# Band attention in a streaming encoder step: more projection steps behind a pair's first scores, a sigmoid gate made from the exponential, the attention outputs stored first

## The chip, the cores and the metric

The kernel runs on one core of one Trainium2 chip. The metric is the device time of the program in microseconds (us), as the median of the runs shown. The program is one launch that evaluates two encoder layers; the change touches one stage of it, the band attention of layer 0, which fills about 855 us of the span.

## The reference, cut to what matters

Layer 0 projects the normalised input to a mixer A (gated DeltaNet) and a mixer B (band attention). Only mixer B is touched:

```python
q_b = rms_norm(q_b.reshape(n_b, L, 16, 64), b_q_g)
k_b = rms_norm(k_b.reshape(n_b, L, 16, 64), b_k_g)
# a frame reads its own chunk of 64 and the 8 chunks before it
o_b = softmax(q k^T / 8 + bias(relative distance)) v
o_b = o_b.reshape(n_b, L, B_W) * jax.nn.silu(z_b)
# outputs also: the last 512 rows of k_b and v_b (and the 32 new rows of the sample group)
```

There are 1024 prompt frames and 32 sample frames (1056 columns in all), everything in float32. silu(z) is z / (1 + exp(-z)).

## The kernel before, in words

`band(...)`  works on 8 pairs of heads, `pair(n, p, more)`, with two sets of buffers (`p` is 0 or 1). While TensorE does the attention of pair n it also computes the projections of pair n+1. The two kinds of work are woven together by hand:

- The attention of a pair has 17 units (`UNITS`), one for each chunk of 64 queries and one for the sample group. For a unit u TensorE does `scores(u)` (q k^T into PSUM tile `SC`), later `turn(u)` (transposes of the softmax weights `E` into `PT`, and into `PX` if there are five blocks), and one unit later `values(u)` (into `PX`).
- VectorE does `negate(u)` (bias added, running minimum, into `NS`; L1862), `weigh(u)` (a reciprocal of the row sums, L1878, and the scaling of `E`, L1880) and `gate(u)` (the product of the attention output with the gated `zs`, written to `OF`; L1900). ScalarE does `soften(u)` (the exponential, L1749) and `copy_turned(u)` (PSUM to SBUF, L1759).
- The projections are a list of 39 jobs, `STREAM`: 28 products (names P1, P5, P6, P3, P7, P2, P4 in this order, for query/key (x=0) and gate/value (x=1), each in two halves of the columns), and the transposes and sums `ck`, `n`, `ko`, `vt`. A product has four steps, another job one step: 123 steps a pair. Each step issues two matmul records in the profile. The jobs use two PSUM banks in turn, so a job may begin only when the job two before it has been evicted: `evicted(pe, n, m - 2)`. P1, P5, P6 and P4 are evicted by ScalarE (L1681), P3, P7 and P2 are added by VectorE (L1805).
- TensorE takes steps of this list by `fill(k)`: `FIRST` steps behind each of the first two scores (3 and 3), then `FILL` in each unit (2 behind the transposes, 2 behind the next scores, 2 behind the values). What is left over is done at the end of the pair. ScalarE and VectorE follow the same counts through `steps_at(u)`, so that each evicts a job where TensorE has passed it.
- ScalarE's `gate(n, p)` (L1731) applies Silu to `zs[p]` (128x1056) when the last projections of pair n have been evicted, ahead of that pair's first `soften`. Silu is in another table set than Exp, so a table is loaded before and after it (L1731, L1732).
- TensorE's code is written out for all pairs. ScalarE runs pairs 1 to 6 as a loop of three turns of two pairs, VectorE and SyncE (SP) pairs 1 to 4 as a loop of two turns; SP's queue issues all DMA of the stage.
- SP's order for pair n, in `follow` and `pair`: the next weights of x=0 after P4 of (0,1), bias and cached keys, the next weights of x=1 after P4 of (1,1), the stores of keys (two DMAs, L1459 and L1460) and values (two, L1462 and L1463), then the store of `OF` (L1471), then the cached values. VectorE's `gate(0)` of the next pair waits for the store of `OF` (`st_o`).

Of the kernel before, what the change touches and what calls it, by code (L numbers as in the profile page):

```python
# [15 lines left out]
NTOK = NP + NS  # L16
# [1241 lines left out]
def band(nc, ident, ones, eps, hT, W, w_ld, w_in, q_g, k_g, rel_bias, cache_k, cache_v, bias_rows,  # L1258
# [6 lines left out]
    with ExitStack() as ctx:  # L1265
# [51 lines left out]
        t_made, w_made, padded = sem("t_made"), sem("w_made"), sem("padded")  # L1317
        z_ok, bias_ok = sem("z_ok"), sem("bias_ok")
        s_done, ns_ok, e_ok, ri_ok, p_ok = sem("s_done"), sem("ns_ok"), sem("e_ok"), sem("ri_ok"), sem("p_ok")
# [24 lines left out]
        NORMS = 5  # L1344
        T_FIRST, T_OPS = {"P5": 2, "P6": 3, "P7": 1, "P4": 4}, 9

# [34 lines left out]

        FIRST, FILL, FILL_LAST = (3, 3), (2, 2, 2), (2, 2, 1)

        def steps_at(u, fill=FILL):

            return sum(FIRST) + sum(fill) * u

# [26 lines left out]
        with nc.Block() as block:  # L1414
            @block.sync
            def _(sp):
# [14 lines left out]
                def follow(n, p, more):  # L1431
                    sp.wait_ge(proj_done, n * J + place["P4", (0, 1)] + 1)
                    for j in (0, 1):
                        if more:
                            load_w(n + 1, j)
                        elif more is False:
                            early_w(sp, W, early_ld, w_out, j, BAND_SLOT[j])
                    if more:
                        sp.wait_ge(bias_ok, n + 1)
                        load_bias(n + 1)  # L1440
                        load_keys(n + 1)
                    sp.wait_ge(proj_done, n * J + place["P4", (1, 1)] + 1)
                    for j in (2, 3):
                        if more:
                            load_w(n + 1, j)
                        elif more is False:
                            early_w(sp, W, early_ld, w_out, j, BAND_SLOT[j])
                    if more is False:
                        early_rows = o_dram.rearrange("(k p) t -> p k t", p=128)
                        sp.dma_start(o_rest, early_rows[:, FIRST_K:H_A - 1, 0:384]).then_inc(eo_ld[0][1], 16)  # L1450
                        for c in (1, 2):
                            c0, w = EARLY_PARTS[c]
                            sp.dma_start(o_parts[c - 1], early_rows[:, 0:H_A - 1, c0:c0 + w]).then_inc(eo_ld[c][0], 16)
                        sp.wait_ge(normed, PAIRS * NORMS)
                        for i in range(2):
                            early_x(sp, x_dram, x_stage, x_ld, i)
                    evicted(sp, n, place["ko", 1])
                    cols = ds(n * 128, 128)
                    sp.dma_start(k_p[:, cols].rearrange("(m p) d -> p m d", p=128), KO[:, 0:4, :]).then_inc(st_k, 16)  # L1459
                    sp.dma_start(k_s[:, cols], KO[0:NS, 4, :]).then_inc(st_k, 16)  # L1460
                    evicted(sp, n, J - 1)
                    sp.dma_start(v_p[:, cols].rearrange("(m p) d -> p m d", p=128), VT[p][:, 4:8, :]).then_inc(st_v, 16)  # L1462
                    sp.dma_start(v_s[:, cols], VT[p][0:NS, 8, :]).then_inc(st_v, 16)  # L1463

                def pair(n, p, more, values):
                    if more is not None:
                        follow(n + 1, 1 - p, more)
                    sp.wait_ge(of_ok, n * UNITS + UNITS)
                    if not values and more is None:
                        return  # L1470
                    sp.dma_start(o_dram[ds(n * 128 + 1024, 128), :], OF[:, :]).then_inc(st_o, 16)  # L1471
                    if values:
                        load_values(n + 2, p)
# [14 lines left out]
                sp.dma_start(o_dram[128 * H_A - 128:128 * H_A, :], o_last[:, 0:NTOK]).then_inc(st_last, 16)  # L1488
                follow(0, 0, True)
                pair(0, 0, True, True)  # L1490
                with sp.Fori(0, 2) as i:
# [18 lines left out]
            def _(pe):  # L1510
                def stream(n, p):

                    for m, (kind, i) in enumerate(STREAM):
                        out = pj[:, (p * J + m) % 2, :]
                        evicted(pe, n, m - 2)
                        if kind in FAST:
                            x, u = i
                            A1, A2 = pair_weights(x)
                            if u == 0:
                                if kind == "P1":  # L1520
                                    pair_loaded(pe, n, x)
                                elif kind in FAST_SUMS:
                                    pe.wait_ge(w_made, n * 8 + x * 4 + FAST_SUMS.index(kind) + 1)
                            if isinstance(n, int) and n == 0 and x == 0:
                                if u == 0 and kind in T_FIRST:
                                    pe.wait_ge(t_made, T_FIRST[kind])
                                elif u == 1 and kind == "P1":
                                    pe.wait_ge(t_made, T_OPS)
                            yield from fast_product(pe, out, lambda name, k: fast_left(A1, A2, S4, name, k),
# [34 lines left out]
                def pair(n, p, more):  # L1564
# [60 lines left out]
                    for u in range(2):  # L1625
                        scores(u)
                        fill(FIRST[u])
                    for u in range(UNITS + 1):
# [22 lines left out]
            def _(act):  # L1651
# [17 lines left out]
                def take(n, p, m):  # L1669
# [4 lines left out]
                    if kind in FAST:  # L1674
                        x, u = i
                        if u == 0 and kind == "P1":
                            if x:
                                wait(act, of_ok, (n - 1) * UNITS)
                            else:
                                wait(act, normed, n * NORMS)  # L1680
# [46 lines left out]

                def gate(n, p):

                    last_of(1, 1, n, act)  # L1730
                    act.activation(zs[p][:, :], zs[p][:, :], ACT.Silu).then_inc(z_ok, 1)  # L1731
                    act.preload_act_table_set("natural_log_exp_and_others")  # L1732

                def pair(n, p, more):
# [27 lines left out]
                    jobs(FIRST[0])  # L1762
                    soften(1)
                    for u in range(UNITS):
                        jobs(steps_at(u))
                        copy_turned(u)
                        jobs(steps_at(u) + FILL[0])
                        if u + 2 < UNITS:
                            soften(u + 2)
                    jobs(1000)  # L1770
                    if more:
                        gate(n + 1, 1 - p)

                act.preload_act_table_set("natural_log_exp_and_others")
                for m in BY_ACT:
                    if m == place["n", 0]:
                        act.wait_ge(consts, 2)
                    take(0, 0, m)
                gate(0, 0)
                pair(0, 0, True)  # L1780
# [6 lines left out]
            def _(dve):  # L1787
# [57 lines left out]
                def pair(n, p, more, again=True):  # L1845
# [67 lines left out]
                    for u in range(UNITS + 1):  # L1913
                        adds(steps_at(u, FILL_LAST))
                        jobs(steps_at(u))
# [5 lines left out]
                        if u + 2 < UNITS:  # L1921
                            negate(u + 2)
                        jobs(steps_at(u) + FILL[0] + FILL[1])
                        if u:
# [6 lines left out]
                for u in range(2):  # L1931
# [10 lines left out]
                    if u == 0:  # L1942
                        combine(0, 0, 2)
                        combine(0, 0, 3)
                    dve.wait_ge(t_made, turn + 3)
                    dve.tensor_tensor(TX[:, 2, :, c0:c1], hT[:, 4:8, c0:c1], TX[:, 0, :, c0:c1], ALU.subtract).then_inc(t_made, 1)
                    turn += 4
                dve.tensor_copy(TX[:, 0, :, SPLIT:WIDE], TX[:, 1, :, SPLIT:WIDE]).then_inc(t_made, 1)
                dve.memset(vraw[:, NTOK:PAD], 0.0).then_inc(padded, 1)
# [1712 lines left out]
```

## Time and profile before

| what | value |
|---|---|
| median of 3 runs (lowest, highest) | 3443.94 us (3440.12, 3444.21) |
| the profiled execution: its time | 3446.64 us |
| the profiled execution: its span, first to last instruction | 3444.9 us |
| granted TensorE clock, mean of the span | 0.991 |
| PE busy (matmuls) | 3353.5 us, 97% of the span |
| DVE, ACT, POOL busy | 1377.8, 1120.7, 502.9 us |
| the band stage in the span | from about 920 to about 1769 us |

PE is TensorE's matmul, PEld its weight load, DVE VectorE, ACT ScalarE, POOL GpSimd, SPq the DMA queue that SP issues. A row of the timeline gives the start, the duration, the engine, the line, the operation with its output and input tiles, and in brackets how long the engine was idle before it and what ended the idle time. The busy time of PE is modelled, so the stage is read here by idle times and by the distance between equal points of successive pairs.

### The profile page before, as it was taken

What the parts mean: (1) busy time and instruction counts of PE and PEld (TensorE: products, weight loads), DVE (VectorE), ACT (ScalarE), POOL (GpSimd) and SP (SyncE); (2) the same over time, 40 slices, a digit from 0 to 9 for tenths busy, and PEclk for the clock granted to TensorE, in tenths of its full rate; (3) what the DMA queues carried; (4) which work ended last, traced back from release to release, by engine and by line L of the source; (5) the groups of instructions that cost most, each with busy time, mean ns of one, the idle gap of its engine ahead of it and who ended that gap; (6) DMA issues with size and microseconds to landing.
All of it is one profiled execution on the core that took longest, in us unless ns stands there. A gap on an engine that the chain in (4) does not pass through costs nothing. (4 is left out here: it accounts for less than half of the span.)

```text
span 3444.9 us, 47339 instructions
## 1 busy us (share of the span) xinstructions
PE 3353.5 (97%) x16261; PEld 2582.4 (75%) x16261; DVE 1377.8 (40%) x3354; ACT 1120.7 (33%) x2862; POOL 502.9 (15%) x506
## 2 busy tenths in 40 slices
PE   8999999999899999999999999899999999999999
PEld 5777777777578878778766667688888888666676
DVE  3555555555344444444320224334333333220233
ACT  4344333343244434334310133123332233210241
POOL 2354345445000000000001001100000000010000
PEclk9999999999999999999999999999999999999999
DMA  6212142112331223222362101111111111470101
GB/s 165 52 38 39 32 23 35 33 32 94 101 46 40 48 48 24 43 48 53 118 204 73 37 1 38 52 50 55 54 42 54 33 45 53 138 234 31 37 1 51
DMA packets 245833, 205.97 MB, mean 60 GB/s; under 512 B 20143, under 2 KB 222799, under 8 KB 245671
## 3 DMA queue, kind: packets, MB, share of 16 engines
q1 hardware_dynamic: 240318, 194.29, 23.5%
q10 hardware_dynamic: 5360, 9.67, 0.7%
q8 instruction: 90, 1.47, 0.2%
q14 instruction: 65, 0.53, 0.1%
HBM read 157.95 MB, written 45.99 MB: 59 GB/s over the span
## 5 line engine op out<-in xcount | busy, mean ns | idle before, releaser
L510 PE MATMUL gdn_pj<-hT,Wb 128*128 128x352 f32 x1536 | 515.0, 461 | 1.6 <-PEq L45 1.6
L510 PEld LDWEIGHTS gdn_pj<-hT,Wb 128*128 128x128 f32 x1536 | 265.5, 191 | 90.3 <-issue 3.2
L2025 PE MATMUL gla_pj<-gla_TX,gla_S 128*128 128x256 f32 (+1 forms) x736 | 191.2, 393 | 0.0
L2025 PE MATMUL gla_pj<-hT,gla_S 128*128 128x256 f32 (+1 forms) x736 | 187.2, 393 | 0.0
L1749 ACT ACTIVATE band_E<-band_NS,band_nm 128x576 f32<-128x576 f32 (+9 forms) x136 | 89.7, 660 | 253.5 <-DVE band_nm L1862 247.4
L2025 PEld LDWEIGHTS gla_pj<-hT,gla_S 128*128 128x128 f32 x736 | 139.4, 190 | 26.2
L2025 PEld LDWEIGHTS gla_pj<-gla_TX,gla_S 128*128 128x128 f32 x736 | 138.2, 190 | 26.2
L1621 PEld LDWEIGHTS band_PX<-band_ET,band_VT 128*128 128x128 f32 x976 | 129.3, 192 | 27.8 <-issue 18.0
L1216 POOL TENSOR_TENSOR x_kept<-gdn_AT,gdn_level 128x384 f32<-128x384 f32 x144 | 144.2, 1032 | 35.7 <-DVE gdn_TT L998 18.5
L2025 PE MATMUL band_pj<-hT,Wb 128*128 128x256 f32 x512 | 141.3, 393 | 5.7 <-DVE band_raw L1805 2.3
L2025 PE MATMUL band_pj<-hT,band_S 128*128 128x288 f32 (+1 forms) x512 | 142.6, 398 | 0.0
L2025 PE MATMUL band_pj<-band_TX,band_S 128*128 128x288 f32 (+1 forms) x512 | 142.4, 399 | 0.2
L1621 PE MATMUL band_PX<-band_ET,band_VT 128*128 128x128 f32 x976 | 131.8, 276 | 8.3 <-DVE band_OF L1900 7.3
L3458 DVE TENSOR_TENSOR fin_xT<-fin_xT,fin_ps 128x384 f32<-128x384 f32 (+1 forms) x48 | 24.6, 519 | 271.0 <-PE fin_ps L3136 239.9
L3195 PE MATMUL fin_ps<-hT,Wb 128*128 128x384 f32 (+1 forms) x384 | 127.4, 467 | 0.0
L3204 PE MATMUL fin_ps<-fin_R,fin_Wx 128*128 128x384 f32 (+1 forms) x384 | 123.0, 463 | 2.2 <-DVE fin_xT L3495 2.1
L1862 DVE CUSTOM_DVE_ANT_0 band_NS<-band_SC,band_bias 128x576 f32<-128x576 f32 (+9 forms) x136 | 83.0, 610 | 105.1 <-issue 104.3
L2025 PE MATMUL gla_pj<-hT,Wb 128*128 128x256 f32 x480 | 119.1, 379 | 0.0
L3168 PE MATMUL fin_ps<-hT,fin_Wq 128*128 128x384 f32 (+1 forms) x384 | 117.2, 459 | 0.0
L3136 PE MATMUL fin_ps<-hT,Wb 128*128 128x384 f32 (+1 forms) x384 | 115.9, 459 | 0.0
L3563 POOL TENSOR_TENSOR fin_acc<-fin_acc,fin_sq 128x384 f32<-128x384 f32 (+1 forms) x42 | 39.0, 929 | 524.7 <-ACT fin_sq L3312 524.5
L1591 PE MATMUL band_SC<-band_KN,band_Qz 128*128 128x288 f32 (+3 forms) x448 | 115.5, 375 | 0.0
(498 smaller groups left out, 6526.1 us busy)
## 6 DMA issues: line engine op xcount, KB each, us to landing
Wb<-in_l_w_in_dram SPq DMA_DIRECT2D x95, 512.0 KB, 7.9
fin_xT<-x_features SPq DMA_DIRECT2D x16, 528.0 KB, 7.9
fin_R<-o_features SPq DMA_DIRECT2D x16, 528.0 KB, 9.7
Wb<-in_l_w_mkv_dram SPq DMA_DIRECT2D x8, 1024.0 KB, 5.4
Wb<-in_l_w_out_dram SPq DMA_DIRECT2D x16, 512.0 KB, 4.3
o_features<-gla_OF ACTq DMA_DIRECT2D x14, 528.0 KB, 7.4
gla_Wv<-in_l_w_in_dram SPq DMA_DIRECT2D x7, 1024.0 KB, 5.4
gdn_GB<-gate_rows SPq DMA_DIRECT2D x8, 544.0 KB, 3.7
```

The source lines that it names most:

```text
L510: mm = pe.matmul(pj[:, m % 2, 0:w], W[:, j, k, :], hT[:, k, c0:c0 + w], start=k == 0, stop=k == KD - 1)
L1216: pool.tensor_tensor(g3(BT, g), g3(AT, g), mask, ALU.mult).then_inc(masked, 1)
L1591: mm = pe.matmul(out[:, b, 0:w], q, KN[p][:, k0 + w * b:k0 + w * b + w], start=True, stop=True)
L1621: mm = pe.matmul(PX[:, 1, :], v, ET[:, u % 2, 128 * b:128 * b + 128], start=b == 0, stop=b == blocks(u) - 1)
L1749: act.activation(E[:, u % 2, a:a + keys(u)], NS_[:, u % 2, 0:keys(u)], ACT.Exp, scale=-1.0, bias=nm[:, u:u + 1], accum_out=rsum[:, u:u + 1 ...
L1862: dve.tensor_tensor_reduce(by_halves(NS_[:, u % 2, :], u), SC[u % 2][:, 0:len(w), 0:w[0]], by_halves(bias[p], u, at), -1.0, 3e38, ALU.add, ...
L2025: mm = pe.matmul(bank[:, 0:w], left(name, k), right(name, k, unit[0], w), start=name in ("P1", "P5", "P2") and k == 0, stop=k == FAST_K - ...
L3136: mm = pe.matmul(ps[:, 3 * (n % 2) + c, 0:w], weights, src[:, c0:c0 + w], start=i == 0, stop=i == len(tiles) - 1)
L3168: mm = pe.matmul(ps[:, i % 3, 0:w], Wqt[:, h, k, :], hT[:, k, c0:c0 + w], start=k == 0, stop=k == KD - 1)
L3195: mm = pe.matmul(out[:, 0:w], Wz[:, x, k, :], hT[:, k, c0:c0 + w], start=k == 0, stop=k == KD - 1)
L3204: mm = pe.matmul(out[:, 0:w], Wo[:, k, 128 * x:128 * x + 128], O[:, k, c0:c0 + w], start=k == 0, stop=k == M_H - 1)
L3563: pool.tensor_tensor(acc[:, part_of(c)], acc[:, part_of(c)], sq[:, a % 2, 0:w], ALU.add).then_inc(acc_ok, 1)
```

## The change

- `FIRST` becomes (6, 6): six steps of the next pair's projections behind each of the first two scores. The last pair, which has other work to fill with, keeps (3, 3) as `FIRST_LAST`. The steps left over at the end of a pair go from nine to three.
- The Silu of `zs` and its two table loads are gone. In their place: ScalarE writes exp(-z) into `vraw` behind the second `soften` (`open_gate`), adds one to it behind the first `copy_turned` (`add_one`, Identity with a bias); VectorE takes the reciprocal of it in unit 0 behind `negate(2)` (128x1056), and in unit 1 behind `negate(3)` multiplies `zs` by it (128x1056).
- SP stores `OF` ahead of the four stores of keys and values, and loads the next weights of x=1 between the stores of keys and those of values (`follow_values`).
- At the start of the stage TensorE's waits for the combined inputs `TX` (`T_FIRST`) are given for each product of both halves, and one small copy is made a little earlier.

```diff
-        T_FIRST, T_OPS = {"P5": 2, "P6": 3, "P7": 1, "P4": 4}, 9
+        T_FIRST = [{"P5": 2, "P6": 3, "P7": 1, "P4": 4}, {"P5": 6, "P6": 8, "P7": 5, "P4": 9}]
...
-        FIRST, FILL, FILL_LAST = (3, 3), (2, 2, 2), (2, 2, 1)
+        FIRST, FILL, FIRST_LAST, FILL_LAST = (6, 6), (2, 2, 2), (3, 3), (2, 2, 1)
...
                     sp.wait_ge(proj_done, n * J + place["P4", (1, 1)] + 1)
-                    for j in (2, 3):
-                        if more:
-                            load_w(n + 1, j)
-                        elif more is False:
+                    if more is False:
+                        for j in (2, 3):
                             early_w(sp, W, early_ld, w_out, j, BAND_SLOT[j])
...
+                def follow_values(n, p, more):
                     evicted(sp, n, place["ko", 1])
                     cols = ds(n * 128, 128)
                     sp.dma_start(k_p[:, cols].rearrange("(m p) d -> p m d", p=128), KO[:, 0:4, :]).then_inc(st_k, 16)
                     sp.dma_start(k_s[:, cols], KO[0:NS, 4, :]).then_inc(st_k, 16)
                     evicted(sp, n, J - 1)
+                    if more:
+                        for j in (2, 3):
+                            load_w(n + 1, j)
                     sp.dma_start(v_p[:, cols].rearrange("(m p) d -> p m d", p=128), VT[p][:, 4:8, :]).then_inc(st_v, 16)
                     sp.dma_start(v_s[:, cols], VT[p][0:NS, 8, :]).then_inc(st_v, 16)
...
                     sp.dma_start(o_dram[ds(n * 128 + 1024, 128), :], OF[:, :]).then_inc(st_o, 16)
+                    follow_values(n + 1, 1 - p, more)
                     if values:
                         load_values(n + 2, p)
...
                     for u in range(2):
                         scores(u)
-                        fill(FIRST[u])
+                        fill((FIRST if more else FIRST_LAST)[u])
...
                             if x:
                                 wait(act, of_ok, (n - 1) * UNITS)
+                                wait(act, z_ok, n * 1)
...
-                def gate(n, p):
+                def open_gate(n, p):
 
                     last_of(1, 1, n, act)
-                    act.activation(zs[p][:, :], zs[p][:, :], ACT.Silu).then_inc(z_ok, 1)
-                    act.preload_act_table_set("natural_log_exp_and_others")
+                    act.wait_ge(proj_done, n * J + J)
+                    act.activation(vraw[:, 0:NTOK], zs[p][:, :], ACT.Exp, scale=-1.0).then_inc(z_exp, 1)
+
+                def add_one(n):
+
+                    act.wait_ge(z_exp, n * 2 + 1)
+                    act.activation(vraw[:, 0:NTOK], vraw[:, 0:NTOK], ACT.Identity, bias=ones[:, 0:1]).then_inc(z_exp, 1)
...
                     soften(1)
+                    open_gate(n, p)
                     for u in range(UNITS):
                         jobs(steps_at(u))
                         copy_turned(u)
+                        if u == 0:
+                            add_one(n)
...
                     jobs(1000)
-                    if more:
-                        gate(n + 1, 1 - p)
...
                         if u + 2 < UNITS:
                             negate(u + 2)
+                        if u == 0:
+                            dve.wait_ge(z_exp, n * 2 + 2)
+                            dve.reciprocal(vraw[:, 0:NTOK], vraw[:, 0:NTOK]).then_inc(z_inv, 1)
+                        elif u == 1:
+                            dve.wait_ge(z_inv, n + 1)
+                            dve.tensor_tensor(zs[p][:, :], zs[p][:, :], vraw[:, 0:NTOK], ALU.mult).then_inc(z_ok, 1)
                         jobs(steps_at(u) + FILL[0] + FILL[1])
```

## Rows read from the trace of the kernel before

**Rows 1.** Busy time by windows, each from one pair's first transposes to the next's.

```profile
core 0: us, PE busy (x) PEld busy (x) DVE busy (x) ACT busy (x) POOL busy (x), PEclk, DMA share, GB/s
991.71:1086.61 94.90, 92.31 (x510) 77.88 (x511) 46.40 (x165) 39.94 (x93) 1.15 (x1) 1.00 0.22 40
1086.61:1181.76 95.15, 92.25 (x509) 77.87 (x509) 46.44 (x165) 39.93 (x93) 1.15 (x1) 1.00 0.22 43
...
1278.42:1376.54 98.12, 95.21 (x509) 80.01 (x510) 46.36 (x165) 39.93 (x93) 1.15 (x1) 0.97 0.31 32
1376.54:1485.57 109.03, 94.57 (x510) 79.34 (x511) 46.31 (x165) 39.93 (x93) 1.15 (x1) 0.95 0.29 52
1485.57:1582.52 96.95, 94.05 (x510) 79.29 (x510) 46.37 (x165) 39.93 (x93) 1.15 (x1) 0.98 0.19 33
```

**Rows 2.** Waits of PE from 930 to 1770 us: total, times, longest.

```profile
PE band_PT L1601 <- DVE band_E L1880: 18.3, 7, 6.1
PE band_PX L1621 <- DVE band_OF L1900: 7.3, 1, 7.3
```

**Rows 3.** Timeline at a pair's start without a loop's jump (1177 to 1182 us).

```profile
1177.09 1.28 ACT L1731 ACT_TABLE_LOAD   x1
...
1178.38 1.08 ACT L1731 ACTIVATE band_zs<-band_zs 128x1056 f32<-128x1056 f32 x1
...
1179.49 1.28 ACT L1732 ACT_TABLE_LOAD   x1
...
1181.76 0.33 PE L1601 MATMUL band_PT<-ident,band_E 128*128 128x128 f32 x1 [1.76 <-DVE band_E L1880]
```

**Rows 4.** Timeline at three later places where PE stands still.

```profile
1278.42 0.48 PE L1601 MATMUL band_PT<-ident,band_E 128*128 128x128 f32 x1 [3.32 <-DVE band_E L1880]
...
1381.71 2.58 SPq L1471 DMA_DIRECT2D o_features<-band_OF  x1
...
1392.30 0.46 DVE L1900 TENSOR_TENSOR band_OF<-band_PX,band_zs 64x64 f32<-64x64 f32 x2 [9.69 <-DMA o_features<-band_OF]
...
1392.90 0.77 PE L1621 MATMUL band_PX<-band_ET,band_VT 128*128 128x128 f32 x2 [7.27 <-DVE band_OF L1900]
...
1484.58 0.35 ACT L1749 ACTIVATE band_E<-band_NS,band_nm 128x64 f32<-128x64 f32 x1 [4.39 <-issue]
...
1485.57 0.47 PE L1601 MATMUL band_PT<-ident,band_E 128*128 128x128 f32 x1 [6.14 <-DVE band_E L1880]
```

**Rows 5.** Small operations of DVE by source line: ns min/median/max.

```profile
L1878 DVE RECIPROCAL band_rinv<-band_rsum x136: 102/164/165, 991.2 to 1754.3; 128x1 f32<-128x1 f32 x136
...
L3515 DVE RECIPROCAL fin_rinv<-fin_rsum x36: 146/155/167, 2017.7 to 3395.8; 128x2 f32<-128x2 f32 x32, 32x2 f32<-32x2 f32 x4
...
L976 DVE RECIPROCAL gdn_kin<-gdn_kin x8: 215/216/217, 119.1 to 822.4; 128x9 f32<-128x9 f32 x8
...
L1017 DVE TENSOR_SCALAR gdn_epsq<-gdn_qss x8: 165/166/168, 156.9 to 862.7; 128x9 f32<-128x9 f32 x8
```

**Rows 6.** Timeline behind the first transposes of pair 2 (they start at 1181.76).

```profile
1182.13 0.28 ACT L1759 ACTIVATE band_ET<-band_PT 128x128 f32<-128x128 f32 x1 [0.26 <-PE band_PT L1601]
...
1183.33 0.35 DVE L1862 CUSTOM_DVE_ANT_0 band_NS<-band_SC,band_bias 128x192 f32<-128x192 f32 x1 [1.20 <-issue]
...
1185.82 0.59 PE L1591 MATMUL band_SC<-band_KN,band_Qz 128*128 128x256 f32 x2
```

**Rows 7.** Operations of the wanted kinds and widths, by source line and by form.

```profile
L2586 ACT ACTIVATE gla_tmp<-gla_X,gla_gbc x8: 1140/1140/1142, 2273.3 to 2954.6; 128x1056 f32<-128x1056 f32 x8
...
L2731 DVE SCALAR_TENSOR_TENSOR gla_QG<-gla_raw,gla_tmp x8: 1251/1258/1259, 2285.6 to 2970.6; 128x1056 f32<-128x1056 f32 x8
...
L1805 DVE TENSOR_TENSOR band_raw<-band_raw,band_pj 128x256 f32<-128x256 f32 x29 | 12.2, 421 | 10.6 <-PE band_pj L2025 10.2
```

**Rows 8.** Timeline of the last pair, third score and third transposes.

```profile
1679.88 0.35 DVE L1862 CUSTOM_DVE_ANT_0 band_NS<-band_SC,band_bias 128x192 f32<-128x192 f32 x1 [1.93 <-issue]
...
1685.62 0.44 PE L1601 MATMUL band_PT<-ident,band_E 128*128 128x128 f32 x2
```

**Rows 9.** Next weights of x=1: their first reader on DVE, and SP's key stores.

```profile
1211.52 0.68 DVE L2108 TENSOR_TENSOR band_S<-Wb 128x512 f32<-128x512 f32 x1
...
L1459 SPq DMA_DIRECT2D out_dram<-band_KO x8: 442/2927/5057, 985.2 to 1677.7; - x8
```

More of the change, by code:

```diff
@@ L1317, in band @@
         t_made, w_made, padded = sem("t_made"), sem("w_made"), sem("padded")
-        z_ok, bias_ok = sem("z_ok"), sem("bias_ok")
+        z_exp, z_inv, z_ok, bias_ok = sem("z_exp"), sem("z_inv"), sem("z_ok"), sem("bias_ok")
         s_done, ns_ok, e_ok, ri_ok, p_ok = sem("s_done"), sem("ns_ok"), sem("e_ok"), sem("ri_ok"), sem("p_ok")
@@ L1380, in target, with steps_at @@
             return lambda f: (raw[:, f, :] if x == 0 else (zs[p], vraw)[f])
-        FIRST, FILL, FILL_LAST = (3, 3), (2, 2, 2), (2, 2, 1)
-        def steps_at(u, fill=FILL):
-            return sum(FIRST) + sum(fill) * u
+        FIRST, FILL, FIRST_LAST, FILL_LAST = (6, 6), (2, 2, 2), (3, 3), (2, 2, 1)
+        def steps_at(u, first=FIRST, fill=FILL):
+            return sum(first) + sum(fill) * u
         def keys(u):
@@ L1442, in follow @@
                     sp.wait_ge(proj_done, n * J + place["P4", (1, 1)] + 1)
-                    for j in (2, 3):
-                        if more:
-                            load_w(n + 1, j)
-                        elif more is False:
+                    if more is False:
+                        for j in (2, 3):
                             early_w(sp, W, early_ld, w_out, j, BAND_SLOT[j])
-                    if more is False:
                         early_rows = o_dram.rearrange("(k p) t -> p k t", p=128)
@@ L1489, in _ @@
                 follow(0, 0, True)
+                follow_values(0, 0, True)
                 pair(0, 0, True, True)
@@ L1523, in stream @@
                                     pe.wait_ge(w_made, n * 8 + x * 4 + FAST_SUMS.index(kind) + 1)
[L1524 to L1528, printed above, removed]
+                            if isinstance(n, int) and n == 0 and x == 0 and kind in T_FIRST[u]:
+                                pe.wait_ge(t_made, T_FIRST[u][kind])
                             yield from fast_product(pe, out, lambda name, k: fast_left(A1, A2, S4, name, k),
@@ L1778, in _ @@
                     take(0, 0, m)
-                gate(0, 0)
                 pair(0, 0, True)
@@ L1913, in pair @@
                     for u in range(UNITS + 1):
-                        adds(steps_at(u, FILL_LAST))
+                        adds(steps_at(u, FIRST_LAST, FILL_LAST))
                         jobs(steps_at(u))
@@ L1944, in _ @@
                         combine(0, 0, 3)
+                    else:
+                        dve.tensor_copy(TX[:, 0, :, SPLIT:WIDE], TX[:, 1, :, SPLIT:WIDE]).then_inc(t_made, 1)
                     dve.wait_ge(t_made, turn + 3)
@@ L1947, in _ @@
                     turn += 4
-                dve.tensor_copy(TX[:, 0, :, SPLIT:WIDE], TX[:, 1, :, SPLIT:WIDE]).then_inc(t_made, 1)
                 dve.memset(vraw[:, NTOK:PAD], 0.0).then_inc(padded, 1)
```

## The prediction

> **What bounds the kernel now.** I read the windows first, then the waits of TensorE, then the timeline. The windows from one pair's first transposes to the next pair's [rows 1] show TensorE's matmuls busy for 92.3 of 94.9 us. A pair costs the time of its matmuls plus TensorE's idle time, and a change here can win only what TensorE stands still, and can lose by making it stand still. The two undisturbed pairs take 94.90 and 95.15 us, 95.0 in the mean, and three take 98.12, 109.03 and 96.95.
>
> The waits [rows 2] name two kinds. Seven times (pairs 0 to 6) the first transposes wait for the softmax weights, 18.3 us in all; once the first values wait 7.3 us for `OF`. The timeline says why. At a pair's start [rows 3] ScalarE loads a table (1.28), does the Silu (1.08) and loads the other table (1.28); the first `soften` stands behind that, and TensorE has 1.76 us of nothing. This occurs five times alike. At pair 3 it is 3.32 and at pair 5 it is 6.14 [rows 4], where ScalarE's loop jumps back and its first `soften` comes another 4.39 us late with "issue" as the only reason. The 7.27 us are a store: it was issued at 1381.71, VectorE waited for it until 1392.30, and TensorE for VectorE.
>
> These waits have an echo. After the 3.32 the pair takes 98.12, so 3.1 us more than 95.0. The window of 109.03 holds the 7.27 and the 6.14, which is 4.38 more than the usual 1.76: 109.03 - 95.0 - 7.27 - 4.38 = 2.4 us more. The one after the 6.14 takes 1.95 more. In these three windows the granted clock falls to 0.95 to 0.98 from 1.00 [rows 1], so matmuls run at the lower level for a while after each such stop. The echo of a stop of over 3 us is 1.95 to 3.1 us, 2.5 in the mean; the 1.76 us stops have none.
>
> **What the change removes.** With six steps behind each of the first two scores, TensorE has about 3.1 us more (six steps of 0.52) ahead of its first transposes, and ScalarE 3.64 us less to do before the first `soften`. Either is more than 1.76, so the five short stops go. At the loop jumps, 4.39 us of issue remain possible, against some 7 us from the first scores to the first transposes; the transposes are safe, but ScalarE also evicts P1, and P3 and P6 now stand ahead of the transposes or near them. I charge 1 us over the stage for that (0 to 3). The store of `OF` is issued when `of_ok` comes, ahead of four other stores, of which the first alone kept SP for 2.9 us in the median [rows 9], and not behind the pair's last evictions; `gate(0)`, which waits for it, comes later than before. The 7.3 us go. Removed: 18.3 + 7.3, and the echoes 3.1 + 2.4 + 1.95, in all 33.0 us.
>
> **What it costs nothing.** The two ScalarE passes over 1056 columns cost 1.08 to 1.14 us each [rows 3, 7]; the exponential lies where ScalarE has three microseconds of slack, the addition of one ends before the reciprocal can start or very nearly. The next weights of x=1 are issued later, behind the store of `OF` and two stores of keys (0.4 to 5.1 us each for the first [rows 9]); their first reader stood at 1211.5, some 35 us into the pair, so up to 15 us late does no harm. The wait of P1 (x=1) for `z_ok`, the finer waits for `TX` and the small copy lie where TensorE is not held by them: nothing. Were the weights' cover gone, products of x=1 would wait for a load.
>
> **The reciprocal.** This is the term that decides. VectorE now takes a reciprocal of 128x1056 in every pair. Before, the trace has reciprocals of one, two and nine elements only [rows 5]: 164, 155 and 216 ns in the median. From one to nine elements is 52 ns for eight, 6.5 ns an element. A TENSOR_SCALAR of nine elements takes 166, so the reciprocal takes 50 ns more for nine, 5.6 above the 1 ns or less that a column costs others (1258 ns for 1056 [rows 7]). From two to nine it is 61 ns for seven, 8.7 an element. For 1056 columns these give 0.16 + 1055 x 0.0065 = 7.0 us, and as bounds 6.4 (6.1 an element) and 9.3. An ordinary pass would be 1.26 [rows 7]; the row of nine, with a spread of 215 to 217, speaks against that. I take 7.0, from one tile's kind of use to the longest row there is.
>
> The Trainium skill, page "VectorE: DVE Perf Modes", section "Walkthrough: the 8-slice pipeline in each mode", says that the reciprocal is a hardware divide repeated eight times per element, and "Trainium Kernel Development and Optimization", section "NeuronCore Architecture", gives VectorE 0.96 GHz. By that rule the pass would be an estimated 8.8 us and not 7.0, and the whole change some 13 us dearer than my sum. The rows lie on the same side, between six and nine times an ordinary column.
>
> **Who waits for it.** The reciprocal stands behind `negate(2)` and ahead of the addition of P3. TensorE may not start P2 (step 21) before P3 has been added (two banks), and then wants `weigh(2)` as well. Let the first transposes start at T, measured on pair 2, where T is 1181.76 [rows 6]. `copy_turned` began 0.37 after T; with P6's eviction ahead of it, it ends at T + 0.85, and `add_one` (1.14) at T + 2.0. `negate(2)` ends at T + 1.9. So the reciprocal runs from T + 2.1 to T + 9.1, the addition of P3 (0.42 [rows 7]) and the handing over end at T + 9.6. TensorE meanwhile does steps 13 to 20, two scores and the second transposes; those are as many steps as lay between the same scores before, and they end with `scores(3)` at 1186.41, T + 4.65. It stands still for 4.95 us. That is over 3 us, so the echo of 2.5 comes with it: 7.45 us in each of pairs 0 to 6, 52.2 us. Behind it VectorE has `weigh(2)`, P7, `negate(3)`, the product (1.26) and `gate(0)`, about 3.3 us, while TensorE at the lower clock has five microseconds of work before `values(1)` wants that gate: no second stop.
>
> In the last pair the fills are other work, and `turn(2)` is what waits. `negate(2)` ended at 1680.23 and the third transposes began at 1685.62 [rows 8]. With 7.0 the reciprocal ends at 1687.3; an addition of 384 columns and `weigh(2)` follow, some 1.0 us together by the 0.42 of 256 columns [rows 7], 1688.3: 2.7 us.
>
> **The sum.** 52.2 + 2.7 + 1.0 - 33.0 = 22.9 us slower. The profiled execution took 3446.64, so it would take 3469.5; that execution lay 2.7 above the median, so the median goes from 3443.94 to 3467. With the lower bounds (6.4 us, echo 1.95) a pair loses 4.35 + 1.95 = 6.3: 44.1 + 2 - 33.0 is 13 slower, 3457. With the upper ones (9.3, 3.1) it loses 7.25 + 3.1 = 10.35: 72.5 + 5 + 3 - 33.0 is 47 slower, 3491.
>
> **The rivals.**
> 1. The reciprocal runs like an ordinary pass, and the 50 ns of the nine-element row are a start-up cost. Then it takes about 1.3 us, ends at T + 3.4, P3 is added before T + 4.65, and TensorE never waits: 33.0 less about 1 for the jumps, 3412. For it: no row has a wide reciprocal, and the one-element rows reach down to 102 ns, so their base is not firm. Against it: the nine-element row is 50 ns above its equal. It decides where 7 x (r - 2.05 + 2.5) + 3 falls below 32, which is a reciprocal r of 3.7 us, 3.5 ns an element. Chance 0.10.
> 2. The reciprocal is about that dear, 3.2 to 4.5 us, and the stop in each pair eats what the removed ones gave, within 7 us of no change: 3437 to 3451. Only a mixture of base and slope would do that. Chance 0.05.
> 3. The loop jumps stay in the path: ScalarE's late start behind the jump, 4.39 us at pair 5, meets the `OF` store and the weights, which now come at the same time, and holds P1's eviction and so P6. A stop of 3 to 5 us with its echo, once or twice, adds 6 to 13 us to my sum: 3473 to 3480. For it: the weights move toward the jump. Against: TensorE has twice the cover. Chance 0.10.
>
> **The numbers.** My forecast, blocked by the reciprocal and without rival 3, has 0.75. It and rival 3 are slower, 0.85, with a little left for losses that I don't see and gains that I don't: slower 0.84, same 0.05, faster 0.11. A difference of 0.2%, 6.9 us, is about what can be told from none here. The forecast's own range is 3457 to 3491; the range for 8 in 10 is 3452 to 3493, which takes in rival 3 and leaves rivals 1 and 2 outside.
>
> **What would show it.** Right: seven reciprocals of 128x1056 of about 7 us; TensorE waiting for VectorE's addition to `raw` (P3, L1805's group) some 5 us in each pair, behind the fourth scores; windows between pairs of about 100.5 us at a clock below 1; the waits for `band_E` at the first transposes gone, the wait for the store gone, no Silu and no table loads in the stage. Wrong: a reciprocal under 4 us, or TensorE going through step 21 without a gap. If the reciprocal is long and the time is still shorter, then the addition of P3 does not hold P2, and I have misread the two banks.

## The result, and the profile after

The changed kernel takes 3469.55 us in the median (3468.51 to 3471.36), beside 3444.07 for the kernel before in the same measurement: 1.0077 times as long, 95% interval 1.0062 to 1.0092, so 25.5 us slower. The prediction said 3467 and 22.9 slower. One execution of experiment 11, 3528.18 us at a granted clock of 0.944, is in a slower state than all others and is left out.

The page of the profiled execution, span and busy shares:

```profile
span 3467.5 us, 47370 instructions
...
PE 3360.6 (97%) x16261; PEld 2586.0 (75%) x16261; DVE 1439.8 (42%) x3370; ACT 1107.9 (32%) x2854; POOL 502.9 (15%) x506
```

VectorE is 62 us busier. TensorE's waits in the band stage (line, what ended the wait, us in total, times, longest), in place of [rows 2]:

```profile
PE band_pj L2039 <- DVE band_raw L1812: 35.9, 8, 6.4
...
PE band_PT L1602 <- DVE band_E L1887: 2.0, 1, 2.0
PE band_PT L1602 <- ACT band_ET L1766: 1.8, 1, 1.8
```

The waits for softmax weights at the first transposes (18.3) and for the store of `OF` (7.3) are gone, and a new one, for VectorE's addition, is by far the largest: one of the eight, 1.3 us, is the start of the stage, where the kernel before had 2.3; the other seven are one for each of pairs 0 to 6. The 2.0 us is the last pair's third transposes. (The stop at the start says nothing about the finer waits for `TX`: over all kernels here it is 1.2 to 2.6 us with them, and 1.5 in experiment 6 without them.) The timeline of pair 2, whose first transposes start at T = 1191.07:

```profile
1191.55 0.27 ACT L1766 ACTIVATE band_ET<-band_PT 128x128 f32<-128x128 f32 x1
1191.71 1.18 ACT L1739 ACTIVATE band_vraw<-band_vraw,ones 128x1056 f32<-128x1056 f32 x1
...
1192.58 0.35 DVE L1869 CUSTOM_DVE_ANT_0 band_NS<-band_SC,band_bias 128x192 f32<-128x192 f32 x1 [2.55 <-issue]
...
1192.92 6.75 DVE L1932 RECIPROCAL band_vraw<-band_vraw 128x1056 f32<-128x1056 f32 x1
...
1194.21 1.03 PE L2039 MATMUL band_pj<-band_TX,band_S 128*128 128x256 f32 x4
...
1195.07 0.59 PE L1592 MATMUL band_SC<-band_KN,band_Qz 128*128 128x256 f32 x2
...
1199.59 0.36 DVE L1812 TENSOR_TENSOR band_raw<-band_raw,band_pj 128x256 f32<-128x256 f32 x1
...
1200.00 1.98 PE L2039 MATMUL band_pj<-hT,Wb 128*128 128x256 f32 x4 [4.34 <-DVE band_raw L1812]
```

The reciprocal starts at T + 1.85, ends at T + 8.6, P3 is added, and TensorE, which was ready at T + 4.6 behind the fourth scores, goes on at T + 8.93. Four of its matmul records then take 1.98 us; in front of the stop, at the higher clock, four took 1.03. Pairs 3 and 5 are worse, with 6.44 us each, and the reason is an old one in a new place:

```profile
1499.27 0.28 ACT L1766 ACTIVATE band_ET<-band_PT 128x128 f32<-128x128 f32 x1 [3.98 <-issue]
...
1499.69 0.30 PE L1602 MATMUL band_PT<-ident,band_E 128*128 128x128 f32 x1 [1.79 <-ACT band_ET L1766]
...
1500.64 6.75 DVE L1932 RECIPROCAL band_vraw<-band_vraw 128x1056 f32<-128x1056 f32 x1 [4.06 <-ACT band_vraw L1739]
...
1507.73 2.08 PE L2039 MATMUL band_pj<-hT,Wb 128*128 128x256 f32 x4 [6.44 <-DVE band_raw L1812]
```

ScalarE is late by "issue" behind its loop's jump, as at this pair before [rows 4]. It is late twice now: by 2.70 us of idle time at the first `soften`, which the six steps cover, and by 3.98 at `copy_turned(0)`. ("Issue" alone is not lateness: VectorE has 2.55 us of it in front of the row at 1192.58, as in other plain pairs. On ScalarE, idle time by issue of over 1.5 us stands nowhere but at pairs 3 and 5, the loop's jumps, in any kernel here.) `add_one`, the reciprocal and TensorE come late with it. The windows from one pair's first transposes to the next's (columns as in [rows 1]; five of seven are shown):

```profile
989.84:1089.54 99.70, 94.29 (x510) 79.14 (x509) 54.05 (x166) 38.42 (x91) 1.15 (x1) 0.98 0.22 41
1191.07:1291.19 100.12, 94.47 (x511) 78.99 (x510) 54.13 (x166) 38.20 (x91) 1.15 (x1) 0.98 0.20 42
1393.70:1494.71 101.01, 95.36 (x510) 79.87 (x509) 54.05 (x166) 38.20 (x91) 1.15 (x1) 0.97 0.28 43
1494.71:1598.78 104.07, 94.16 (x510) 78.92 (x509) 54.16 (x166) 38.31 (x91) 1.15 (x1) 0.97 0.21 41
1598.78:1698.56 99.78, 93.89 (x498) 77.54 (x497) 51.55 (x162) 37.70 (x89) 0.00 (x0) 0.97 0.19 54
```

Each is longer than the undisturbed 95.0 of before, and none of the seven has a full clock.

### The profile page after: what moved, and what is told of

Same layout as the page of the kernel before. It is cut to its first block and busy times, and to the rows that moved or that the text cites. A ratio compares the mean times of both kernels' runs of the same rounds, so it can differ in the third digit from the quotient of the medians.

```text
span 3467.5 us, 47370 instructions
## 1 busy us (share of the span) xinstructions
PE 3360.6 (97%) x16261; PEld 2586.0 (75%) x16261; DVE 1439.8 (42%) x3370; ACT 1107.9 (32%) x2854; POOL 502.9 (15%) x506
## 5 line engine op out<-in xcount | busy, mean ns | idle before, releaser
L2039 PE MATMUL band_pj<-hT,Wb 128*128 128x256 f32 x512 | 150.2, 415 | 40.4 <-DVE band_raw L1812 35.9
L2039 PEld LDWEIGHTS band_pj<-hT,Wb 128*128 128x128 f32 x512 | 99.1, 207 | 65.6 <-DVE band_raw L1812 39.1
```

Source lines behind the costliest of these rows:

```text
L2039: mm = pe.matmul(bank[:, 0:w], left(name, k), right(name, k, unit[0], w), start=name in ("P1", "P5", "P2") and k == 0, stop=k == FAST_K - ...
```

## The experiments

Each timed kernel is compared with the kernel before on the same chip (median 3443 to 3445 us). Differences between experiments that ran on different chips carry that spread of 2 us.

**1. The old gate back.** ScalarE's Silu with its two tables, the rest of the change kept.

```diff
-                    open_gate(n, p)
...
-                            add_one(n)
...
                     jobs(1000)
+                    if more:
+                        gate(n + 1, 1 - p)
...
-                            dve.reciprocal(vraw[:, 0:NTOK], vraw[:, 0:NTOK]).then_inc(z_inv, 1)
```

> The changed kernel with the old gate: Silu and its two table loads ahead of a pair's first soften, no exponential, no reciprocal; six steps behind the first scores and the new order of the stores stay. Theory (the reciprocal is the whole loss): the waits for P3's addition vanish, 34.6 us of stops with their echoes; what the steps and the stores win remains, less a stop at P6 where P1's eviction now waits for the table loads: about 0.3 us in plain pairs and 2 and 4.5 us at the two loop jumps. About 3423 us (3415 to 3430). Rival (the loss comes from the six steps or from the new order of DMAs): the time stays within 7 us of the changed kernel's 3469.5.

Measured: 3425.89 us, 0.9940 of before (0.9923 to 0.9956). The steps and the order of the DMAs are not the loss; the gate is: with it the same kernel is 43.7 us longer. TensorE stands seven times about 0.7 us at P6 (4.8 in all), and once 2.3 at pair 5.

**2. A cheap pass in the reciprocal's place.** The division is left out.

```diff
-dve.reciprocal(vraw[:, 0:NTOK], vraw[:, 0:NTOK]).then_inc(z_inv, 1)
+dve.tensor_scalar(vraw[:, 0:NTOK], vraw[:, 0:NTOK], 0.5, None, ALU.mult).then_inc(z_inv, 1)
```

> The changed kernel with the reciprocal of 128x1056 replaced by a multiplication by 0.5 in the same place with the same waits: the division of the gate is left out, nothing else. Theory (it is the length of the reciprocal, 6.75 us, and nothing about its place or its waits): the pass takes 0.8 to 1.3 us, VectorE adds P3 before TensorE asks, all seven stops and their echoes go: about 3414 us (3409 to 3420). Rival (the extra waits between ScalarE and VectorE cost the time, whatever the pass): 3455 us or more.

Measured: 3421.38 us. The pass takes 0.71 us, the seven stops at P3 are gone, and the 48.2 us between this and the changed kernel hang on the length of one instruction. It is 7 us above the expected 3414 and 1.4 above the range: one stop of 3.31 us with its echo is left at pair 5, where ScalarE is idle for 5.50 us by issue.

**3. The sigmoid on ScalarE alone.** exp(-ln(1 + exp(-z))); VectorE keeps the product.

```diff
-act.activation(vraw[:, 0:NTOK], vraw[:, 0:NTOK], ACT.Identity, bias=ones[:, 0:1]).then_inc(z_exp, 1)
+act.activation(vraw[:, 0:NTOK], vraw[:, 0:NTOK], ACT.Ln, bias=ones[:, 0:1]).then_inc(z_exp, 1)
...
+                    act.wait_ge(z_exp, n * 2 + 2)
+                    act.activation(vraw[:, 0:NTOK], vraw[:, 0:NTOK], ACT.Exp, scale=-1.0).then_inc(z_inv, 1)
...
-                            dve.reciprocal(vraw[:, 0:NTOK], vraw[:, 0:NTOK]).then_inc(z_inv, 1)
```

> The changed kernel with the sigmoid made on ScalarE alone, with functions of the table set that is loaded anyway: exp(-z) behind the second soften, Ln with a bias of one behind the first copy_turned, exp(-x) behind the third soften; VectorE keeps only the product. Theory: ScalarE has the room for a third pass of 1.1 us in unit 0, so as without the division: about 3414 us (3409 to 3422). Rival (ScalarE is late now: the third pass holds the next copy_turned and TensorE stands at the second or third transposes, seven times over 1 us): 3425 us or more.

Measured: 3419.14 us, 0.9925 of before (0.9908 to 0.9941), 5 above the expected 3414 and inside the range. The passes take 1.07, 1.18 and 1.07 us and hold nobody in plain pairs. One stop of weight is left, at pair 5, behind ScalarE's loop jump; experiment 9 takes it away with the passes unchanged:

```profile
1466.08 0.28 ACT L1771 ACTIVATE band_ET<-band_PT 128x128 f32<-128x128 f32 x1 [5.69 <-issue]
...
1466.50 0.44 PE L1602 MATMUL band_PT<-ident,band_E 128*128 128x128 f32 x1 [3.51 <-ACT band_ET L1771]
```

**4. P3's addition ahead of the reciprocal.**

```diff
+                        jobs(steps_at(u) + FILL[0] + FILL[1])
                         if u == 0:
                             dve.wait_ge(z_exp, n * 2 + 2)
                             dve.reciprocal(vraw[:, 0:NTOK], vraw[:, 0:NTOK]).then_inc(z_inv, 1)
...
-                        jobs(steps_at(u) + FILL[0] + FILL[1])
```

> The changed kernel with the same reciprocal moved one place, behind the addition of P3 in unit 0. Theory (P3's addition holds P2 by the two banks, and the third transposes stand next, since their softmax weights are scaled behind the reciprocal): the waits for P3's addition vanish, TensorE stands instead at the third transposes waiting for band_E for 3.2 us in each of seven pairs, so 1.1 us less than 4.34: about 3460 us (3450 to 3465). If a stop so short has a smaller echo, 3450. Rival (it is not the banks but the product or the gate behind the reciprocal that TensorE waits for): no change, 3469.

Measured: 3459.83 us. The waits for P3 vanish and TensorE stands at the third transposes, as expected, 3.4 us in a plain pair (expected 3.2):

```profile
1198.16 0.44 PE L1602 MATMUL band_PT<-ident,band_E 128*128 128x128 f32 x2 [3.43 <-DVE band_E L1887]
1198.49 1.13 PE L2039 MATMUL band_pj<-band_TX,Wb 128*128 128x256 f32 x4
```

Pair 5 has a further 3.70 us at the second transposes, behind the loop jump, and three pairs have 1.2 us more behind ScalarE's eviction. So the two banks are what holds TensorE in the changed kernel, and the softmax weights of unit 2 come next.

**5. The reciprocal in six slices.** 176 columns in each of units 0 to 5; the product is sliced with it, one unit later, and each gate waits for its slices only (cut here to the reciprocal).

```diff
-                            dve.reciprocal(vraw[:, 0:NTOK], vraw[:, 0:NTOK]).then_inc(z_inv, 1)
+                            if u < PARTS_Z:
+                                part = slice(WZ * u, WZ * u + WZ)
+                                dve.reciprocal(vraw[:, part], vraw[:, part]).then_inc(z_inv, 1)
```

> The changed kernel with the reciprocal and the product in six slices of 176 columns, one slice in each of units 0 to 5 (its product one unit later), each gate waiting for its slices only. Same columns divided in all. Theory (6.75 us is 0.16 and 6.2 ns a column, and what hurts is that it lies in one piece ahead of P3): a slice takes 1.25 us, which VectorE has in each unit, so the stops at P3 go: 3419 us (3414 to 3425), as the version with Ln and Exp. Rival (VectorE's time in the first units is itself what TensorE lacks, in slices or in one): TensorE stands over 0.5 us in most of the first six units, 3432 us or more.

Measured: 3420.75 us, 0.9929 of before (0.9916 to 0.9943).

```profile
L1941 DVE RECIPROCAL band_vraw<-band_vraw x48: 1244/1247/1254, 993.5 to 1677.6; 128x176 f32<-128x176 f32 x48
```

Six slices are 7.5 us of VectorE in a pair, more than the 6.75 of the one piece, and cost TensorE nothing in plain pairs (93.45 to 93.8). What hurt is not the amount of work, but that it lay in one piece ahead of what TensorE wanted.

**6. Only the six steps, on the kernel before.**

```diff
-        FIRST, FILL, FILL_LAST = (3, 3), (2, 2, 2), (2, 2, 1)
+        FIRST, FILL, FIRST_LAST, FILL_LAST = (6, 6), (2, 2, 2), (3, 3), (2, 2, 1)
```

> The kernel before with the six steps behind each of the first two scores and nothing else: Silu with its tables and the old order of the stores stay. Theory: the stops at the first transposes go but for short ones at P6 and one at the loop jump, as in the run with the Silu kept; the wait for the store goes too, since gate(0) stands six steps later and the store is issued before the same steps: 3427 us (3420 to 3434). Rival (the store's order is what removed the 7.3 us): 3434 to 3438 us, with one stop of 5 to 7 us at the first values.

Measured: 3439.74 us, 0.9987 of before (0.9978 to 0.9997): neither theory. The stops at the first transposes are gone, but pairs 3 and 5 stop at P6 for 3.30 and 4.33 us behind ScalarE's late start, and the store is waited for all the same:

```profile
1386.65 0.50 PE L1621 MATMUL band_PX<-band_ET,band_VT 128*128 128x128 f32 x2 [5.03 <-DVE band_OF L1900]
...
1477.90 3.78 PE L2025 MATMUL band_pj<-band_TX,band_S 128*128 128x256 f32 x8 [4.33 <-ACT band_raw L1681]
```

**7. Only the gate** (and the finer waits at the start). The changed kernel with `FIRST` (3, 3) and the old order of SP (cut here to the first).

```diff
-        FIRST, FILL, FIRST_LAST, FILL_LAST = (6, 6), (2, 2, 2), (3, 3), (2, 2, 1)
+        FIRST, FILL, FIRST_LAST, FILL_LAST = (3, 3), (2, 2, 2), (3, 3), (2, 2, 1)
```

> The changed kernel with three steps behind each of the first two scores and the old order of SP: of the change only the gate by exponential and reciprocal (and the finer waits at the start) is left. Theory: with six steps less behind it, TensorE has P3 and the first half of P7 still to issue when the reciprocal begins, so it comes to the third transposes before it needs the sum of P3; it stands there for 2.2 us in each of seven pairs and not 4.34: 3438 us (3430 to 3446). The reciprocal and the six steps are dear only together. Rival (the reciprocal costs the same 50 us wherever TensorE's steps stand): 3470 us or more.

Measured: 3459.03 us, 1.0048 of before (1.0032 to 1.0063). The place is the theory's, third transposes, but the time is 13 us above the range: a plain stop is 2.88 and not 2.2 us, and the old order brings the loop jumps (6.3 us once) and the store (4.4 us) back, which I had left out:

```profile
PE band_PT L1598 <- DVE band_E L1883: 29.2, 10, 6.3
PE band_PX L1618 <- DVE band_OF L1903: 4.4, 1, 4.4
```

"Dear only together" is too strong: the gate alone costs 15 us. Yet the parts do not add up either. With three steps the windows of pairs 0 and 1 are 96.27 and 97.95 us, with six in the changed kernel 99.70 and 101.53: beside the one-piece reciprocal the six steps, which were to win time, cost 3.4 and 3.6 us in these pairs, because they bring TensorE to the bank that waits for P3.

**8. Only the order of SP** (and the finer waits at the start), Silu and three steps kept: experiment 1 with `FIRST` (3, 3).

> The kernel before with the new order of SP's stores and weights and the finer waits at the start; Silu and three steps stay. Theory: only the wait for the store of OF and its echo go, 7.3 and 2.4 us: 3435 us (3431 to 3440), with the seven stops at the first transposes as before. Rival (that wait came by chance in the profiled execution and is no part of the median): 3444 us.

Measured: 3426.38 us, 0.9950 of before (0.9934 to 0.9965), better than expected by 9 us:

```profile
PE band_PT L1602 <- DVE band_E L1882: 12.3, 7, 1.8
```

All seven stops are now the 1.76 of the table loads, at pairs 3 and 5 too. The new order took away the store's wait and most of what the loop jumps cost; one stop of 2.3 us at pair 5 is left of them:

```profile
1472.34 1.99 PE L2028 MATMUL band_pj<-band_TX,band_S 128*128 128x256 f32 x4 [2.29 <-ACT band_raw L1683]
```

Of the gain, 16.4 us lie between the first transposes of pair 0 and those of pair 7 (669.8 us against 686.2), where the finer waits at the start have no part. The way from the stage's start to pair 0's first transposes is 1.8 us shorter, about what it varies by between kernels that all have the finer waits (1.7 us between experiments 3 and 9).

**9. ScalarE's loop written out**, on experiment 3.

```diff
-                with act.Fori(0, 3) as i:
+                for i in range(3):
                     pair(i * 2 + 1, 1, True)
```

> The version with Ln and Exp, with ScalarE's loop over pairs 1 to 6 written out. Theory (ScalarE's late starts marked issue at pairs 3 and 5 come from the loop's jump, behind which its code must be brought again while the stores and weights fill the DMA engines): no idle of ScalarE by issue over 1 us at those places, the one stop of 3.5 us at the second transposes of pair 5 and its echo of 2 go: 3414 us (3411 to 3417). Rival (the late starts come from the amount of code and not from the jump): they stay or appear at every pair, 3419 us or more.

Measured: 3410.67 us, 0.9907 of before (0.9891 to 0.9922), the fastest version of all and just under the expected 3411 to 3417. ScalarE has no idle time by issue in these pairs, and all of pairs 0 to 5 take the same time (two of the windows):

```profile
1083.51:1176.96 93.45, 92.36 (x511) 77.94 (x510) 47.58 (x165) 39.35 (x92) 1.15 (x1) 1.00 0.21 43
1363.84:1457.29 93.45, 92.36 (x510) 77.94 (x509) 47.58 (x165) 39.34 (x92) 1.15 (x1) 1.00 0.31 46
```

**10. Experiment 3 with three steps.**

```diff
-        FIRST, FILL, FIRST_LAST, FILL_LAST = (6, 6), (2, 2, 2), (3, 3), (2, 2, 1)
+        FIRST, FILL, FIRST_LAST, FILL_LAST = (3, 3), (2, 2, 2), (3, 3), (2, 2, 1)
```

> The version with Ln and Exp with three steps behind each of the first two scores in place of six. Theory (without table loads the softmax weights of unit 0 are ready 2.1 us after the first scores and TensorE comes for them after 3.6; the six steps are worth only what they cover at the loop jumps): plain pairs as with six steps, 93.6 us each; at pairs 3 and 5 ScalarE's late start is covered by 3.1 us less: 3425 us (3419 to 3429). Rival (three steps are too few everywhere): all seven first transposes wait over 0.5 us, 3430 us or more.

Measured: 3420.78 us, beside 3419.14 with six. Plain pairs are 92.9 to 93.9, no longer than with six; the stops at the jumps are 1.80 and 3.77. The time is as expected (3419 to 3429). With the tables gone, the steps earn nothing that can be told.

**11. The weights of x=1 behind all stores**, and **12. at their old place** (both on experiment 3). First 11, then 12, each cut to the lines that are added; the same lines between the stores go:

```diff
                     sp.dma_start(v_s[:, cols], VT[p][0:NS, 8, :]).then_inc(st_v, 16)
+                    if more:
+                        for j in (2, 3):
+                            load_w(n + 1, j)
```

```diff
                     sp.wait_ge(proj_done, n * J + place["P4", (1, 1)] + 1)
+                    for j in (2, 3):
+                        if more:
+                            load_w(n + 1, j)
```

> The version with Ln and Exp with the next weights of x=1 (1 MB) loaded behind all four stores of keys and values and not between them. Theory (what makes ScalarE late at the jumps is the load on the DMA engines, and the weights are its largest part): ScalarE's idle by issue at pair 5 falls under 2.5 us, TensorE's stop of 3.5 us there goes: 3414 us (3411 to 3418). Rival (the stores of single 512 byte rows are what delays it): no change, 3417 to 3422.

> The version with Ln and Exp with the next weights of x=1 at their old place, right behind P4 of (1,1) and ahead of the store of OF; the store of OF is still ahead of the stores of keys and values. Theory (the stores' order, not the weights', removed the wait of gate(0), and early weights have half landed before the jump): within 4 us of the version with Ln and Exp, 3415 to 3423. Rival (the weights' place is what keeps the loop jumps cheap): both jumps cost TensorE 3 us or more with echoes: 3426 us or more.

Measured: 3417.43 us for 11 (the middle of three: 3416.78 to 3422.42), and 3433.62 us for 12 (0.9973 of before, 0.9963 to 0.9983). Later does nothing that can be told: ScalarE still has 5.39 us of idle time by issue at pair 5, and my theory for 11 fell. Earlier costs 14.5 us against experiment 3 and 16.2 against experiment 11, and my theory for 12 fell too, its rival holds: the weights' place, not only the store's, is what the new order wins by. There are three stops. At pair 3 VectorE, whose own loop jumps there, is late, and TensorE stands 3.14 us; at pair 5 it is ScalarE (7.56 us by issue), and TensorE stands 4.53. The one at pair 4 is no jump, it is the wait for the store of `OF`, which is back:

```profile
1273.32 0.06 DVE L1873 MEMSET band_tick<- 128x1 f32 x1 [8.59 <-issue]
...
1274.42 3.48 PE L2043 MATMUL band_pj<-band_TX,band_S 128*128 128x256 f32 x8 [3.14 <-ACT band_raw L1683]
...
1383.31 0.46 DVE L1914 TENSOR_TENSOR band_OF<-band_PX,band_zs 64x64 f32<-64x64 f32 x2 [5.64 <-DMA o_features<-band_OF]
...
1383.91 0.77 PE L1622 MATMUL band_PX<-band_ET,band_VT 128*128 128x128 f32 x2 [3.45 <-DVE band_OF L1914]
```

That store was issued at 1363.42, ahead of the stores of keys and values but right behind the two loads of weights, and took 19.8 us to land. In experiment 3, where the weights come behind it, the same store took 2.8 us.

## Why the prediction was right, and where it was not

**The size of what is removed** was put at 33.0 us. Experiment 9, the stage without any of these stops, is 32.4 us under its kernel before, and from the first transposes of pair 0 to those of pair 7 it takes 33.2 us less (653.0 against 686.2). The sum stands, as what was there to be removed.

**Who removes it** was wrong in two sentences. "The five short stops go" by the six steps: with the Silu kept they only move, from 1.76 us at the first transposes to 0.7 at P6 (experiments 1 and 8: 3425.89 and 3426.38, no difference), because P6 waits until ScalarE, behind the same tables, has evicted P1. What makes those stops go is that the tables go (experiment 10, three steps: no stop over 0.7 us at the first transposes). And the later weights were costed at nothing, and the store's wait was said to go because the store comes ahead of four others; with the weights still ahead of it, it stays (experiment 12; 6 and 7 with the whole old order). The order of SP alone gives 17.3 us, the steps alone 4, and beside the reciprocal the steps cost time (experiment 7).

**The reciprocal** was the term that decides. Taken as 7.0 us from one and nine elements, it measures 6.75:

```profile
L1932 DVE RECIPROCAL band_vraw<-band_vraw x8: 6748/6752/6754, 991.7 to 1700.8; 128x1056 f32<-128x1056 f32 x8
```

With the 1247 ns of 176 columns that is 5505 ns for 880 columns, 6.26 ns each; the rows had given 6.5. (The "1 ns or less" that the prediction gives an ordinary column does not fit its own row: 1258 ns for 1056 is 1.2.) The estimate of 8.8 us from the Trainium skill's "VectorE: DVE Perf Modes" (a divide repeated eight times, section "Walkthrough: the 8-slice pipeline in each mode") was 2 us too long (that section gives the repeats and no time; one cycle for each was the estimate's reading); the measurement decides. Rival 1 is out: experiment 2 is that rival made true, and it gives 3421.38, not 3412, since the jumps still cost.

**Who waits** was right: P3, at step 21, behind the fourth scores, and after it the softmax weights of unit 2 (experiment 4). The plain stop is 4.34 us, not 4.95: the reciprocal starts 0.25 earlier, is 0.25 shorter, and P3's addition overlaps its end.

**The echo** of a stop was put at 2.5 us. With 93.45 us as the undisturbed pair (92.35 for pair 6, as in experiment 9), the echoes of the seven stops are the window less 93.45 less the stop: 1.9 at pair 0, 2.3 at pair 2, 2.4 to 3.7 for the others, 19.2 in all, 2.75 in the mean. A stop of 1.76 has hardly one (experiment 8: 95.1, less 93.17 for a plain pair with three steps as in experiment 10, less 1.76, is 0.2). In experiment 4, less all its stops, the echoes are 0.5 to 3.0.

**The loop jumps** were undersized. I charged 1 us; they cost 2.1 in each of pairs 3 and 5 through the reciprocal's late start, and 1.79 at the second transposes, 6.0 in all. Rival 3 had named a late start there as still in the path, but for the wrong reason: the weights, moved toward the jump, helped (experiment 12).

The terms side by side, predicted and measured: plain stops 34.7 and 30.4; echoes 17.5 and 19.2; jumps 1.0 and 6.0; last pair 2.7 and 2.0; removed 33.0 and 32.4 to 33.2. The sums are 22.9 and 24.4 to 25.2; measured were 25.5. The total was nearly right partly by luck: the errors in stops and jumps have opposite signs.

## What to carry to other kernels

A wide reciprocal on VectorE is several ordinary passes long (6.75 us against 1.25). Where Exp and Ln are loaded anyway, 1/(1 + e) as exp(-ln(1 + e)) on ScalarE cost TensorE nothing here, and neither did the reciprocal in slices between the other work. Before an operation is put on an idle engine, ask which of that engine's next jobs the bound engine wants, and when: VectorE was idle for about half of a pair here (46.4 of 95 us busy [rows 1]), and one piece of 6.75 us still cost TensorE 4.3 us and a slow clock behind it. A change that covers a wait can hurt beside another change: test the parts together and apart. And where hand woven engines run loops beside a written-out one, look at each loop's jump together with the transfers that are issued there; loads of 1 MB put ahead of a store also hold the store.

## What the runs showed of the hardware that was not expected

- Behind a loop's jump an engine can be late by microseconds, and not always at its first instruction. ScalarE's idle time by issue there is 1.57 and 4.39 us before, 2.70 and 3.98 at one pair in the changed kernel, 3.05 and 5.69 in experiment 3, 8.28 in experiment 7; VectorE has 8.59 in experiment 12. Writing ScalarE's loop out removes all of it on ScalarE (experiment 9). That ScalarE's jump is the cause there is shown; VectorE's loop was not written out.
- What is waited for is most likely the code itself. The Trainium skill, "Runtime: NRT & Kernel Launch", section "Instruction fetch mechanics", says that a taken branch outside the buffered code forces a DMA fetch, and the traces agree: their DMA view has packets of kind instruction, and at pair 5, in all thirteen kernels in which ScalarE loops, each of its late operations starts 1.5 to 2.3 us behind the start of a packet of queue q14. In experiment 3 the packets start at 1454.9 and 1464.5, and ScalarE goes on at 1457.21 and 1466.08; in experiment 9 that queue has none between 1384 and 1484. The second packet, in the DMA view from 1464.5 to 1464.6 us (packets, MB, share):

```profile
q14 instruction: 1, 0.01, 19.3%
```

- The packet itself can come late. At pair 5 it starts 0.8 us behind ScalarE's last operation ahead of the jump in experiment 3, and 5.9 us behind it in experiment 12, where the weights were issued earlier. That the weights hold it back fits with this. It is not shown: a packet's row says when it starts, not when it was asked for, and loading the weights after all stores (experiment 11) did not bring the second packet forward, which stays open.
- A stop of TensorE can cost more than its length: matmuls that took 0.26 us a record take 0.5 us for a while behind it (1.98 for four at 1200.00, 1.03 before), the granted clock's lower level, 1.2 GHz against 2.4. Its length alone does not say whether: behind 2.29 us in experiment 8 four records took 1.99 us and the pair lost 2.0 us more, behind 2.87 us at pair 0 of experiment 7 only 0.5 were lost, and behind 3.43 us in experiment 4 four records took 1.13.
- The reciprocal's time hardly varies, 6748 to 6754 ns over eight, and its slope is 6.26 ns a column from 176 to 1056 columns and 6.2 from the 164 ns of one element [rows 5] to 176, as against 1.2 for a product of two tiles (1.25 us for 1056).
